# A hand-ordered three-block transformer program: one piece of filler work of each attention step is put between the turnings and the scores, and small ScalarE operations go behind the copies

## The chip, the cores and the metric

The program runs on one core of a Trainium2 chip. The metric is the device time of one execution in microseconds, less is better. TensorE (PE) does the matrix products, ScalarE (ACT) copies and exponentials, VectorE (DVE) elementwise work and reductions, GpSimd (POOL) a few additions and its own queue of transfers, SyncE (SP) issues the weights' transfers.

## The reference

Sequence 512, width 1024, everything float32. First one block, then twice the same layer:

```
first block:  ffn -> [ local attention (8 heads) | dilated attention (3 groups of 4 heads) ]
              each branch times a gate sigmoid(h @ w_gate), summed, @ w_out -> ffn
layer x 2:    h = rmsnorm(x);  z = h @ w_in
              o_c = causal attention over latents (8 heads)
              o_b = banded attention with sinks (8 heads)
              o_a = g0 * compressed attention + g1 * selected + g2 * window  (8 heads)
              g = sigmoid(h @ w_branch_gate)                      # 3 x 1024 columns
              x += (g_a*(o_a@w_a) + g_b*(o_b@w_b) + g_c*(o_c@w_c)) @ w_out
              ffn, embedding gate; at the end rmsnorm
```

## The kernel before

A planner in Python writes down a list of steps, and each engine's program is made by walking that list: an engine's instructions stand in the order of the steps, and each waits on semaphores for what it reads and for the buffer it writes. So the order in which `go()` and `layer()` call their helpers is the order on every engine.

Products of weights (`dense`) are split in float32r halves: a weight tile of 512 KB comes in on SP's queue into one of three raw tiles, ScalarE writes its high half (the CAST at L1877), VectorE the rest (L2010), into one of four split tiles, and TensorE does three matmuls for each of eight chunks, 24 matmuls of 128x512 (L1691 to L1693). The split of weight unit u+2 is listed with the first matmuls of unit u. Sums stand in PSUM banks: ring `PB` has four, taken in turn, ring `OB` four, taken oldest first.

Attention is done by `attend(slots, fill)`. It goes over pairs of slots; a slot has two batches of heads, so a step has four batches. In step p the old pair is finished and the new pair begun:

```
turn(old)      PE transposes the four score matrices (L1775) into 4 PB banks, ACT copies them out (L1937)
turned, behind things put off from the step before
score(new)     PE products (L1767) into PB banks; DVE adds the mask and takes the peak (L2083), ACT exp (L1929)
value(old)     PE products (L1789)
norm(new)      DVE divides by the sums (L2098 to L2114); the next step's turn waits for it
between(new)   post, pre, and then the step's portion of `fill`
```

The fill is what TensorE does while the softmax of the new pair runs on DVE and ACT: gates of the branch, either whole (`gates`, 24 matmuls) or in quarters (`quarters`, 6 matmuls each). A gate ends in `tangent`: DVE multiplies the bank (L2160), ACT takes the tanh (L1953), POOL's queue stores it to HBM. For a bank of `OB` this is put into `behind`, that is after the next turnings on the list; for a bank of `PB` it follows at once. `roomy()` picks the ring.

The places: local attention (`ga`, 4 steps with turnings, about 448 to 520 us), dilated groups 0, 1, 2 (`gb`, to 700 us), and in each layer the causal attention (whole gates, from 1255 and 2208 us), the band (from 1364 and 2316 us) and the last attention (from 1486 and 2439 us, eleven turnings, here called A1 to A11). In the causal one `heads_in` makes the keys and queries of the next heads in between: three products in three PB banks, copied out by ACT (L1969), and for every other head a rotation, whose first copy is L1966. In the last one `cmp_score` makes the compressed scores of the next query tile: 3 DVE operations, an exp on ACT (L1997), and 4 DVE operations (L2280 to L2286).

Of the kernel before, what the change touches and what calls it, by code (L numbers as in the profile page):

```python
# [159 lines left out]
class Plan:  # L160
# [3 lines left out]
    def __init__(self, nc, D, out):  # L164
# [9 lines left out]
        self.inside = False  # L174
        self.unopened = 0
# [332 lines left out]
    def attend(self, slots, fill=(), at_once=False):  # L508
# [6 lines left out]
        self.inside = True  # L515

# [65 lines left out]
        def between(ss):  # L582
            for f in ss:
                for B in slots[f]:
                    for U in B:
                        if U.get("post"):
                            U["post"]()
            for f in ss:
                for B in slots[f]:
                    for U in B:  # L590
                        if U.get("pre"):
                            U["pre"]()
            for f in next(fill, None) or ():
                f()

        for p in range(len(pairs) + 1):
# [6 lines left out]
            for f in back:  # L603
                f()
            if not new:
                between(())
# [31 lines left out]
    def roomy(self):  # L638
        return self.OB if self.inside and len(self.OB.out) + self.unopened < 3 else self.PB

    def quarters(self, name, ms, H):

        def piece(m, k, held):
            if k == 0:
                ring = self.roomy()
                assert ring is self.OB
# [12 lines left out]
    def tangent(self, name, m, ring, b, bank, tok):  # L659
        def tangent():  # L660
# [3 lines left out]
            self.gate_at[name, m] = (len(self.gate_at), self.load(self.D["gates"][len(self.gate_at)], s[:], (n, "t")))  # L664
            self.tmp.give(i, self.gate_at[name, m][1])
        if ring is self.OB:
            self.behind.append(tangent)
        else:
            tangent()
# [76 lines left out]
    def go(self):  # L746
# [98 lines left out]
        self.attend(self.batches(na_us), [ga[0:2], ga[2:3], ga[3:4], ga[4:6], ga[6:7]])  # L845
# [15 lines left out]
        for g in range(3):  # L861
# [22 lines left out]
            for t, hh in order:  # L884
# [35 lines left out]
            self.attend(self.batches(us), self.portions(*[(gb[0:8], (3, 2, 2, 1)), (gb[8:20], (8, 4)),  # L920
                                                          (gb[20:32], (8, 4))][g]), at_once=g > 0)
# [193 lines left out]
    def layer(self, L, xt, ht):  # L1115
# [100 lines left out]
        us = []  # L1216

        def heads_in(m, later=False, between=None):
# [15 lines left out]
            if m % 2 == 0:  # L1234
                places = to_place[m // 2] = []

                def rotated(d):
                    for f in places:
# [4 lines left out]
                          done=rotated)  # L1243
            got = []
            for R, (b, bank, tok) in ((kf, res[0]), (qf, res[1])):
# [7 lines left out]
                got.append((took, w))  # L1253
            tq = got[1][0]
# [228 lines left out]
        for qt in range(4):  # L1483
            for kind in range(2):
                for h in range(8):
# [4 lines left out]
                    def cmp_scores(qt=qt):  # L1490
# [3 lines left out]
                        OB.give(b, (n, "b"))  # L1494
# [1069 lines left out]
```

## Time and profile before

| | us |
|---|---|
| median of 3 runs | 3093.63 (3093.18 to 3093.67) |
| the profiled execution, its own time | 3091.7 |
| its span, first to last instruction | 3089.5 |
| PE busy | 3020.2 |
| DVE busy | 1672.6 |
| ACT busy | 1203.5 |
| mean granted TensorE clock | 0.996 |

The span is the time between the first and the last instruction; the 2.2 us around it are outside the program. Busy times overlap. In the waits "A <- B: x, n" says that A's engine stood idle for x us over n times until B was done. In a timeline row the bracket gives the idle time of the engine just ahead of the row and what ended it.

### The profile page before, as it was taken

To read this page: it belongs to the slowest core of one execution; us is meant where nothing else is said; L and a number is where in the kernel's file an instruction comes from. 1 tells how busy PE (TensorE), PEld (TensorE's weight loads), DVE (VectorE), ACT (ScalarE), POOL (GpSimd) and SP (SyncE) were. 2 spreads that over 40 slices of the span, in tenths; PEclk is the share of its full clock that TensorE was granted. 3 is DMA by queue.
4 is the path that set the end of the run, shared out by engine and by line. 5 is a ranking of instruction groups with operands and counts; after the bars stand their busy time and mean duration, and the time that the engine had idled before them with its cause. 6 is when DMAs were issued, how large, how long until landed. Compare 5 with 4: busy or idle time off the path is not lost.

```text
span 3089.5 us, 40035 instructions
## 1 busy us (share of the span) xinstructions
PE 3020.2 (98%) x15272; PEld 2478.8 (80%) x15272; DVE 1672.6 (54%) x3050; ACT 1203.5 (39%) x2238; POOL 286.5 (9%) x344
## 2 busy tenths in 40 slices
PE   8999999999999999999999999999999999999998
PEld 7888887888888888778778888888778778888887
DVE  6653364446565426556656555436556666555434
ACT  4322334443432224645553322224546553322223
POOL 0000110001100012011001100013111001100002
PEclk9999999999999999999999999999999999999999
DMA  5333373325233333225225332334223315322332
GB/s 170 113 96 114 108 144 119 103 86 179 95 100 99 96 108 111 73 101 167 73 63 183 97 96 96 96 98 151 87 95 117 127 49 184 103 96 96 102 97 95
DMA packets 105996, 338.15 MB, mean 109 GB/s; under 512 B 15360, under 2 KB 15888, under 8 KB 105680
## 3 DMA queue, kind: packets, MB, share of 16 engines
q1 hardware_dynamic: 84816, 272.45, 28.0%
q0 software_dynamic: 20992, 63.15, 7.0%
q8 instruction: 123, 2.02, 0.3%
q14 instruction: 65, 0.53, 0.1%
HBM read 299.24 MB, written 27.52 MB: 106 GB/s over the span
## 4 chain that ended last, share of the span: by engine, by line
PE 89%; ACT 3%; DVE 3%; issue 2%; DMA 2%; POOL 1%; SPq 0%; POOLq 0%; DVEq 0%; ACTq 0%
PE bk L1691 26%; PE bk L1693 25%; PE bk L1692 25%; PE bk L1767 3%; PE bk L1789 3%; PE bk L1775 1%; PE bk L1730 1%; PE bk L1732 1%; PE bk L1731 1%; ACT t L1929 1%; ACT t L1937 1%; ACT t L1877 1%; DMA t<-value_scratch 0%; DVE t L2160 0%; DVE t L2010 0%
## 5 line engine op out<-in xcount | busy, mean ns | idle before, releaser
L1691 PE MATMUL bk<-t,t 128*128 128x512 f32 x3784 | 1481.0, 391 | 25.1 <-DVE t L2010 13.8
L1693 PE MATMUL bk<-t,t 128*128 128x512 f32 x3784 | 1469.2, 388 | 0.0
L1692 PE MATMUL bk<-t,t 128*128 128x512 f32 x3784 | 1468.3, 388 | 0.0
L1691 PEld LDWEIGHTS bk<-t,t 128*128 128x128 f32 x3784 | 712.6, 188 | 182.1 <-issue 26.2
L1693 PEld LDWEIGHTS bk<-t,t 128*128 128x128 f32 x3784 | 712.5, 188 | 147.3
L1692 PEld LDWEIGHTS bk<-t,t 128*128 128x128 f32 x3784 | 713.1, 188 | 141.9
L2010 DVE TENSOR_TENSOR t<-t,t 128x1024 fp32r<-128x1024 f32 (+3 forms) x538 | 616.7, 1165 | 353.9 <-ACT t L1877 353.2
L1877 ACT CAST t<-t 128x1024 fp32r<-128x1024 f32 (+3 forms) x538 | 511.3, 979 | 217.1 <-PE bk L1693 109.5
L1920 ACT CAST t<-t 128x512 fp32r<-128x512 f32 x88 | 54.6, 621 | 433.7 <-DVE t L2070 433.7
L1929 ACT ACTIVATE t<-t,t 128x256 f32<-128x256 f32 (+3 forms) x336 | 173.1, 516 | 95.8 <-DVE t L2083 94.9
L2316 POOL TENSOR_TENSOR t<-t,t 128x512 f32<-128x512 f32 x58 | 78.3, 1349 | 1387.4 <-ACT t L1907 1387.3
L2067 DVE SCALAR_TENSOR_TENSOR t<-bk,t 128x512 f32<-128x512 f32 x88 | 60.6, 691 | 246.8 <-PE bk L1693 246.7
L2083 DVE CUSTOM_DVE_ANT_0 t<-bk,t 128x256 f32<-128x256 f32 (+3 forms) x272 | 110.2, 456 | 125.3 <-PE bk L1767 77.9
L1903 ACT ACTIVATE t<-t,t 128x512 fp32r<-128x512 f32 x72 | 51.0, 722 | 224.3 <-DVE t L2293 195.1
L1767 PE MATMUL bk<-t,t 64*128 64x256 f32 (+7 forms) x672 | 115.3, 421 | 20.5 <-ACT t L1937 18.4
L1917 ACT ACTIVATE t<-t 128x512 f32<-128x512 f32 x88 | 55.5, 632 | 189.8 <-DVE t L2061 189.8
L1937 ACT COPY t<-bk 128x512 f32<-128x512 f32 (+2 forms) x200 | 95.3, 558 | 64.6 <-PE bk L1775 63.9
L1767 PEld LDWEIGHTS bk<-t,t 64*128 64x128 f32 (+1 forms) x672 | 65.7, 190 | 54.2 <-ACT t L1937 39.2
L2312 POOL DMA_DIRECT2D gate_scratch<-t x64 | 35.3, 552 | 728.1 <-ACT t L1953 563.4
L1789 PEld LDWEIGHTS bk<-t,t 128*64 128x64 f32 x1456 | 79.2, 137 | 24.3 <-issue 23.6
L1775 PE MATMUL bk<-t,t 128*128 128x128 f32 x728 | 90.6, 273 | 5.3 <-ACT t L1969 4.5
L1775 PEld LDWEIGHTS bk<-t,t 128*128 128x128 f32 x728 | 82.0, 140 | 15.4 <-ACT t L1969 5.7
(173 smaller groups left out, 1997.6 us busy)
## 6 DMA issues: line engine op xcount, KB each, us to landing
t<-in_f_g SPq DMA_DIRECT2D x88, 512.0 KB, 4.4
t<-in_f_u SPq DMA_DIRECT2D x88, 512.0 KB, 3.6
t<-in_f_d SPq DMA_DIRECT2D x64, 512.0 KB, 4.3
t<-in_gate SPq DMA_DIRECT2D x48, 512.0 KB, 3.7
gate_scratch<-t POOLq DMA_DIRECT2D x64, 256.0 KB, 2.3
t<-gate_scratch POOLq DMA_DIRECT2D x64, 256.0 KB, 3.7
t<-in_f_d SPq DMA_DIRECT2D x32, 384.0 KB, 3.1
t<-in_wo SPq DMA_DIRECT2D x24, 512.0 KB, 3.7
```

Source lines behind the costliest of these rows:

```text
L1691: pe.matmul(o, wh, xh, start=start, stop=False)
L1692: pe.matmul(o, wh, xl, start=False, stop=False)
L1693: return pe.matmul(o, wl, xh, start=False, stop=stop)
L1767: ins = pe.matmul(b["bank"][:, w["at"]:w["at"] + w["w"]], w["q"], w["k"], start=True, stop=True)
L1775: ins = pe.transpose(b["bank"][:, j * 128:(j + 1) * 128], b["S"][:, j * 128:(j + 1) * 128], P.cn("ident"))
L1789: ins = pe.matmul(v["o"], v["v"][j], b["PT"][:, c:c + 128], start=j == 0 and not v["add"], stop=end, skip_group_check=v["add"])
L1877: e.then_inc(act.copy(P.spl[u % NSPL][:, 0, 0:n], P.raw[u % NRAW][:, 0:n]), "halves", ("hi", u))
L1929: e.then_inc(act.activation(S, S, ACT.Exp, bias=w["nm"], scale=-1.0, accum_out=w["sm"]), "exps", (n, "e", j, i))
L1937: e.then_inc(act.copy(b["PT"][:, 0:b["w"]], b["bank"][:, 0:b["w"]]), "acts", (n, "a", j))
L2010: e.then_inc(dve.tensor_tensor(lo, P.raw[u % NRAW][:, 0:n], hi.bitcast(F32), ALU.subtract), "rests", ("lo", u))
L2083: e.then_inc(dve.tensor_tensor_reduce(b["S"][:, c:c + k], b["bank"][:, c:c + k], w["table"], -w["scale"], w["init"], ALU.add, ALU.min, w[" ...
L2316: e.then_inc(pool.tensor_tensor(P.acc[:], P.acc[:], s["q"][:], ALU.add), "pools", (n, "p"))
```

## The change

Five edits, all of order; no instruction is added or removed.

1. In every step with an old and a new pair and more than one function in its portion, the first function is called between the turnings and the scores. Three calls of `attend` are touched by that (dilated group 0, band, last attention). In groups 1 and 2 one quarter (`lead`) is called ahead of the first scores.
2. `tangent` is two steps now. The DVE product stays where it was; the tanh and the store of a gate in a PB bank go to `behind`, after the next turnings. In the last step (`closing`) a whole gate takes a PB bank.
3. The local attention's portions are 3, 1, 1, 1, 1 gates, before 2, 1, 1, 2, 1.
4. `heads_in` lists its four copies ahead of the rotation's copy.
5. `cmp_score` is two steps: the first (transposes, 3 DVE operations, exp) stands between the norms of the new pair (`later`), the second, `cmp_share`, where all of it was.

```diff
@@ attend
+        for f in lead:
+            f()
...
             for f in back:
                 f()
+            todo = list(next(fill, None) or ())
+            if old and new and len(todo) > 1:
+                todo.pop(0)()
             if not new:
-                between(())
+                self.closing = True
+                between((), todo)
+                self.closing = False
...
             for s in old if not at_once else ():
                 done(s)
+            each(new, "later")
             for s in new[1:2]:
                 norm(s)
             if new:
-                between(new)
+                between(new, todo)
@@ roomy, tangent
-        return self.OB if self.inside and len(self.OB.out) + self.unopened < 3 else self.PB
+        return self.OB if self.inside and not self.closing and len(self.OB.out) + self.unopened < 3 else self.PB
...
             n = self.step("sigmoid", g=bank, tg=tok, s=s, f=f, r=self.rf_tok)
             ring.give(b, (n, "g"))
-            self.gate_at[name, m] = (len(self.gate_at), self.load(self.D["gates"][len(self.gate_at)], s[:], (n, "t")))
-            self.tmp.give(i, self.gate_at[name, m][1])
+
+            def turned():
+                k = self.step("tangent", s=s, t=(n, "g"))
+                self.gate_at[name, m] = (len(self.gate_at), self.load(self.D["gates"][len(self.gate_at)], s[:], (k, "t")))
+                self.tmp.give(i, self.gate_at[name, m][1])
+            if self.inside and ring is self.PB:
+                self.behind.append(turned)
+            else:
+                turned()
@@ calls
-        self.attend(self.batches(na_us), [ga[0:2], ga[2:3], ga[3:4], ga[4:6], ga[6:7]])
+        self.attend(self.batches(na_us), [ga[0:3], ga[3:4], ga[4:5], ga[5:6], ga[6:7]])
...
-            self.attend(self.batches(us), self.portions(*[(gb[0:8], (3, 2, 2, 1)), (gb[8:20], (8, 4)),
-                                                          (gb[20:32], (8, 4))][g]), at_once=g > 0)
+            self.attend(self.batches(us), self.portions(*[(gb[0:8], (3, 2, 2, 1)), (gb[9:20], (7, 4)),
+                                                          (gb[21:32], (7, 4))][g]), at_once=g > 0, lead=[[], gb[8:9], gb[20:21]][g])
@@ heads_in
-            if m % 2 == 0:
+            def turning():
...
+            if m % 2 == 0 and not later:
+                turning()
             got = []
...
                 got.append((took, w))
+            if m % 2 == 0 and later:
+                turning()
```

**The order on ScalarE at the end of the causal attention of layer 0.** The last exponentials of the fifth step, the split of a weight unit, the tanh of the gate, and the copies of the last turnings (tiles `t_76` to `t_79`). Before:

```order
L1929 ACTIVATE t_79,t_66<-t_79,t_66 128x512
L1877 CAST t_58<-t_54 128x1024
L1953 ACTIVATE t_72<-t_72 128x512
L1937 COPY t_76<-bk 128x256
L1937 COPY t_77<-bk 128x256
L1937 COPY t_78<-bk 128x512
L1937 COPY t_79<-bk 128x512
L1923 CAST t_129<-bk 128x4x128 x2
L1877 CAST t_55<-t_52 128x1024
```

Of the change:

```order
L1959 ACTIVATE t_79,t_66<-t_79,t_66 128x512
L1907 CAST t_58<-t_54 128x1024
L1967 COPY t_76<-bk 128x256
L1967 COPY t_77<-bk 128x256
L1967 COPY t_78<-bk 128x512
L1967 COPY t_79<-bk 128x512
L1953 CAST t_129<-bk 128x4x128 x2
L1983 ACTIVATE t_72<-t_72 128x512
L1907 CAST t_55<-t_52 128x1024
```

The tanh has moved from ahead of the four copies to behind them and behind the output's two halves (line numbers differ by 30).

**The order on ScalarE at A1 of layer 0.** The exp of the compressed scores (L1997, then L2027), copies of the turnings, the tanh of the gate finished just before (`t_70`), the split of the unit that belongs to the moved quarter (`t_57`), the new pair's exponentials. Before:

```order
L1997 ACTIVATE t_69<-t_69 128x256
L1877 CAST t_56<-t_54 128x1024
L1937 COPY t_76<-bk 128x512
L1937 COPY t_77<-bk 128x512
L1937 COPY t_78<-bk 128x512
L1937 COPY t_79<-bk 128x512
L1953 ACTIVATE t_70<-t_70 128x512
L1929 ACTIVATE t_74,t_66<-t_74,t_66 128x256 x2
L1929 ACTIVATE t_75,t_66<-t_75,t_66 128x256 x2
L1929 ACTIVATE t_76,t_66<-t_76,t_66 128x256 x2
L1929 ACTIVATE t_77,t_66<-t_77,t_66 128x256 x2
L1923 CAST t_131<-bk 128x4x128
```

Of the change:

```order
L2027 ACTIVATE t_68<-t_68 128x256
L1907 CAST t_56<-t_54 128x1024
L1967 COPY t_76<-bk 128x512
L1967 COPY t_77<-bk 128x512
L1967 COPY t_78<-bk 128x512
L1967 COPY t_79<-bk 128x512
L1983 ACTIVATE t_70<-t_70 128x512
L1907 CAST t_57<-t_52 128x1024
L1959 ACTIVATE t_74,t_66<-t_74,t_66 128x256 x2
L1959 ACTIVATE t_75,t_66<-t_75,t_66 128x256 x2
L1959 ACTIVATE t_76,t_66<-t_76,t_66 128x256 x2
L1959 ACTIVATE t_77,t_66<-t_77,t_66 128x256 x2
```

The CAST of `t_57`, before behind these exponentials and an output, now stands ahead of them. VectorE's rest of `t_57` likewise moves ahead of the peaks.

**The order on TensorE at A2 of layer 0.** The last filler matmuls ahead of the turnings, the turnings, the scores, the compressed values. Before:

```order
L1692 MATMUL bk<-t_50,t_55 128x512
L1693 MATMUL bk<-t_50,t_55 128x512
L1775 MATMUL bk<-t_59,t_74 128x128 x4
L1775 MATMUL bk<-t_59,t_75 128x128 x4
L1775 MATMUL bk<-t_59,t_76 128x128 x4
L1775 MATMUL bk<-t_59,t_77 128x128 x4
L1767 MATMUL bk<-t_149,t_161 128x256 x8
L1861 MATMUL bk<-t_71,t_160 64x128 x8
```

Of the change:

```order
L1805 MATMUL bk<-t_59,t_76 128x128 x4
L1805 MATMUL bk<-t_59,t_77 128x128 x4
L1721 MATMUL bk<-t_50,t_55 128x512
L1722 MATMUL bk<-t_50,t_55 128x512
L1723 MATMUL bk<-t_50,t_55 128x512
L1721 MATMUL bk<-t_50,t_55 128x512
L1722 MATMUL bk<-t_50,t_55 128x512
L1723 MATMUL bk<-t_50,t_55 128x512
L1797 MATMUL bk<-t_149,t_161 128x256 x8
L1891 MATMUL bk<-t_71,t_160 64x128 x8
```

A quarter of a gate, six matmuls, stands between the turnings and the scores; 12 of the 18 filler matmuls remain ahead of the next turnings.

## Rows read from the trace of the kernel before

**Rows 1.** The page's part 1: busy time, share, count of each engine.
```profile
PE 3020.2 (98%) x15272; PEld 2478.8 (80%) x15272; DVE 1672.6 (54%) x3050; ACT 1203.5 (39%) x2238; POOL 286.5 (9%) x344
```

**Rows 2.** Waits of TensorE over the span: engine, line waited for: us, times, longest.
```profile
PE bk L1767 <- ACT t L1937: 18.4, 19, 3.2
...
PE bk L1691 <- ACT t L1923: 5.5, 2, 2.8
```

**Rows 3.** Timeline of one local-attention step; columns: start, us, engine, line.
```profile
461.36 1.91 PE L1775 MATMUL bk<-t,t 128*128 128x128 f32 x16
...
462.29 0.63 ACT L1953 ACTIVATE t<-t 128x512 f32<-128x512 f32 x1 [3.58 <-DVE t L2160]
462.82 2.03 ACT L1937 COPY t<-bk 128x512 f32<-128x512 f32 x4
...
464.02 1.42 PE L1767 MATMUL bk<-t,t 64*128 64x256 f32 x9 [0.75 <-ACT t L1937]
```

**Rows 4.** Timeline where the first step's values wait for their operand.
```profile
470.18 0.66 PE L1789 MATMUL bk<-t,t 128*64 128x128 f32 x8 [2.58 <-DMA t<-value_scratch]
```

**Rows 5.** Windows: length, PE busy (matmuls), granted clock, DMA share, GB/s.
```profile
471.40:474.80 3.40, 3.40 (x10) 0.50 0.28 64
...
1498.80:1505.60 6.80, 5.89 (x36) 0.50 0.34 118
2451.50:2458.30 6.80, 5.88 (x70) 1.00 0.30 116
2198.50:2202.00 3.50, 3.50 (x10) 0.51 0.54 192
1247.40:1250.90 3.50, 3.50 (x17) 1.00 0.61 190
```

**Rows 6.** Timeline of the last causal turning, layer 0.
```profile
1325.82 0.63 ACT L1953 ACTIVATE t<-t 128x512 f32<-128x512 f32 x1 [3.99 <-DVE t L2160]
...
1327.83 1.11 ACT L1923 CAST t<-bk 128x512 fp32r<-128x512 f32 x2
...
1329.27 0.47 PE L1691 MATMUL bk<-t,t 128*128 128x512 f32 x1 [2.77 <-ACT t L1923]
```

**Rows 7.** Timeline of the causal step that has heads_in(2), layer 0.
```profile
1274.76 0.58 ACT L1966 COPY t<-bk 128x512 f32<-128x512 f32 x1 [1.62 <-PE bk L1693]
1275.24 2.44 ACT L1969 ACTIVATE t<-bk 64x512 f32<-64x512 f32 x4
...
1277.78 1.06 PE L1775 MATMUL bk<-t,t 128*128 128x128 f32 x8 [0.60 <-ACT t L1969]
```

**Rows 8.** Timeline at the start of the second dilated group.
```profile
623.83 1.39 PE L1767 MATMUL bk<-t,t 64*128 64x128 f32 x20 [0.73 <-DVE t L2050]
```

**Rows 9.** Timeline of two band steps, layer 0.
```profile
1386.49 1.91 PE L1775 MATMUL bk<-t,t 128*128 128x128 f32 x16
...
1388.35 2.11 PE L1767 MATMUL bk<-t,t 64*128 64x256 f32 x16
...
1397.87 1.91 PE L1775 MATMUL bk<-t,t 128*128 128x128 f32 x16
...
1398.31 0.62 DVE L2112 TENSOR_SCALAR t<-t,t 128x256 f32<-128x256 f32 x2
```

**Rows 10.** Timeline of the first two steps of the last attention, layer 1.
```profile
2449.82 0.42 ACT L1997 ACTIVATE t<-t 128x256 f32<-128x256 f32 x1 [2.84 <-DVE t L2278]
2450.14 1.03 ACT L1877 CAST t<-t 128x1024 fp32r<-128x1024 f32 x1
...
2452.41 2.12 PE L1767 MATMUL bk<-t,t 64*128 64x256 f32 x16 [3.16 <-ACT t L1937]
...
2453.55 0.43 DVE L2083 CUSTOM_DVE_ANT_0 t<-bk,t 128x256 f32<-128x256 f32 x1 [0.17 <-PE bk L1767]
...
2461.29 0.73 DVE L2114 TENSOR_SCALAR t<-t,t,t 128x256 f32<-128x256 f32 x2
```

**Rows 11.** Waits of TensorE, 2440 to 2560 us (last attention, layer 1).
```profile
PE bk L1767 <- ACT t L1937: 5.4, 3, 3.2
```

More of the change, by code:

```diff
@@ L580, in norm, with each, between @@
                 X["p"] = (k, "d")
-        def between(ss):
-            for f in ss:
-                for B in slots[f]:
+        def each(ss, name):
+            for s in ss:
+                for B in slots[s]:
                     for U in B:
[L586 to L593, printed above, removed]
+                        if U.get(name):
+                            U[name]()
+        def between(ss, todo):
+            each(ss, "post")
+            each(ss, "pre")
+            for f in todo:
                 f()
+            todo.clear()
         for p in range(len(pairs) + 1):
@@ L659, in tangent, with left @@
     def tangent(self, name, m, ring, b, bank, tok):
-        def tangent():
+        def left():
             i, s, f = self.tmp.take()
@@ L1494, in cmp_scores, with cmp_shares @@
                         OB.give(b, (n, "b"))
+                        cmp_[qt] = (i, S, n)
+                    def cmp_shares(qt=qt):
+                        i, S, n = cmp_[qt]
+                        n = self.step("cmp_share", qt=qt, S=S, e=(n, "e"), sgs=sgs, sgt=sgt)
                         cmp_[qt] = (i, S, (n, "d"))
@@ L1521, in post, with later @@
                             f_(qt + 1)
+                    def later(qt=qt, kind=kind, h=h, f_=cmp_scores):
+                        if h == 0 and kind == (qt > 0) and qt < 3:
+                            f_(qt + 1)
                     if qt == 0 and kind == 0 and h == 0:
-                        first_scores = cmp_scores
+                        first_scores = (cmp_scores, cmp_shares)
                     def done(tok, es, qt=qt, kind=kind, h=h):
@@ L1542, in layer @@
                                                        for j in range(qt + 1)],
-                        lambda: v_t, h, qt, 0.125, col, open=opn, post=post, done=done, most=4, add=True, gate=gate,
+                        lambda: v_t, h, qt, 0.125, col, open=opn, post=post, later=later, done=done, most=4, add=True, gate=gate,
                         sms=columns(S_SM, col, 1), rss=columns(S_RS, col, 1),
                         o=lambda qt=qt, h=h: half_out(obk[qt][1], h), ot=lambda qt=qt: obk[qt][2]))
-        first_scores()
+        for f in first_scores:
+            f()
         opened[14]()
@@ L2278, in vector @@
             vec(dve.tensor_tensor(S3, S3, mx.unsqueeze(2).broadcast_to([128, 8, 32]), ALU.subtract), (n, "s"))
-            e.wait_ge((n, "e"))
+        elif kind == "cmp_share":
+            qt = s["qt"]
+            S3 = s["S"][:, 0:256].rearrange("p (h n) -> p h n", h=8)
+            some = P.cn("cmp01")[:, qt:qt + 1]
+            sx = P.st[:, 176:184]
+            e.wait_ge(s["e"])
             vec(dve.tensor_reduce(sx, S3, AX, ALU.add), (n, "1"))
```

20 lines of the change are left out of this document (10 added, 10 removed).

## Prediction

> **What bounds the kernel now.** I read the page's busy times first. TensorE is busy 3020.2 of the span of 3089.5 us, VectorE little more than half, ScalarE 39% [rows 1]. So nothing but TensorE's idle time, under 70 us, and stretches at a lower clock can be won by an edit that only changes order. The Trainium skill ("Perfetto Trace Analysis", Identifying the Most-Contended Engine) warns that matmul busy time says little of the distance from the roofline, and names the busy share of the weight loads instead, here 80%. For what order alone can win I keep to the idle time.
>
> Then the waits of TensorE: the largest is 18.4 us in 19 waits, scores (L1767) waiting for ScalarE's copies of the turned scores (L1937), since four turnings fill the four banks of `PB` and the scores need two of them. 5.5 us in two waits are matmuls of L1691 behind an output's split (L1923) [rows 2]. Then the timelines at each place touched.
>
> **How a step is reckoned.** Let s be how much later (plus) or earlier the scores of a step start than before. A moved quarter is 6 matmuls, 1.36 us: 0.227 us from start to start in the fuller timeline, and the window at full clock has 17 in 3.5 us [rows 5]. From start of turnings to start of scores a step takes 1.86 us [rows 9], of which the turnings are 1.64 and the wait and switch 0.22. With a quarter in between, the turnings' end and the scores are 1.50 apart. TensorE then comes to the next turnings 1.36 earlier relative to s. If the norms are ready, that is gain; if not, it waits again. So every moved quarter wins the gap less 0.14, and loses what the next norms are late.
>
> **The terms.**
>
> *Tanh behind the copies.* In a local step the tanh takes 462.29 to 462.82 after waiting for VectorE's product, then come the copies; scores start 2.66 us after the turnings [rows 3], against 1.86 where no tanh stands ahead [rows 9]. That is 0.80 us a step. It holds in three local steps with scores, and in two steps of each causal attention: 7 x 0.8 = 5.6. Ahead of the fourth local turnings' gate I take another 0.3. What is late next are the exponentials, by one tanh; they have cover, since these steps still have a whole gate, 24 matmuls, ahead of the next turnings.
>
> *The last gate of the causal attention.* The gate waits 2.77 us for the output's split, which frees an `OB` bank; that split starts at 1327.83 behind tanh and copies [rows 6]. In a `PB` bank it needs only the first copy. 2.8 a layer, 5.6.
>
> *The rotation behind the four copies.* ScalarE sits idle 1.62 us until the third product ends, copies it, and only then spends 2.44 us on the four copies of the first two; the turnings wait, at the last 0.60 us, for those banks [rows 7]. Moved ahead, two copies fall into that idle time. The third bank comes free last, with one copy of 0.58 and a product on VectorE of about the same, so I count 1.4 a layer, 2.8.
>
> *Three gates in the first local step.* The values of the next step waited 2.58 us for `value_scratch`, until 470.18 [rows 4]. With one gate more ahead of them, 5.45 us, they come later than that. Right behind the wait the granted clock was 0.50 for 3.4 us [rows 5], which cost about 1.5. Together 4.1. The fourth step loses the gate, where the norms have been ready 7 us before; no loss.
>
> *Leads.* The first scores of groups 1 and 2 wait 0.73 for a product on VectorE [rows 8]; covered: 1.5.
>
> *Dilated group 0.* Gaps of 0.45 give s = +1.1, then +0.9; the third turnings' norms, ready now just in time, are then late. Net loss 0.4.
>
> *Band.* Here gaps are 0.22, so s = +1.3. At the second turnings VectorE had been busy until the scores and takes up 1 us of that. At the third it had waited for them: all 1.2 us of delay arrive. The last norm there runs 1398.31 to 1398.93, its turnings begin 1.3 us after 1397.87 [rows 9], so there were 0.25 us of slack. The turnings end 1.0 late, and after the last moved quarter 0.9 is left: loss 1.8 in two layers.
>
> *Last attention.* Scores wait 5.4 us a layer for copies, the longest 3.2 [rows 11]; with waits too short for that view the gaps are 8.1, less 10 x 0.14: 6.7 could be won. At A1 the exp of the compressed scores starts at 2449.82, after all norms, a cast of 1.03 follows, then the copies; scores only at 2452.41 [rows 10]. Now the exp can start near 2447.2; the three operations put between the norms cost the last norm about 1.0 and the turnings' end 0.5; scores start near 2451.0, s = -1.4. But VectorE's rest of the moved quarter's weight unit stands ahead of the peaks, and waits for the chain product L2160 (end 2452.5), tanh 0.6, cast 1.0; with its own 1.15 the peaks start at 2455.3, before at 2453.55. From there to the end of the last norm, 2461.29 + 0.73 [rows 10], were 8.5 us, 1.5 of them a wait for values which now is gone, so about 7.4: 2462.7. TensorE is at the turnings near 2458.9, waits in between them, and ends them where it did, -0.15. The gain of A1 is eaten. A2: s = +1.1, plus three compressed operations between the norms: A3's turnings end 0.9 late; its gap of 1.9 gives s = +0.5. A4 to A10 win their gaps, but at A6 the norms are 0.65 late, since a weight unit's split was moved ahead of the peaks at A5. Sum at A11: -1.8 a layer, 3.6. In layer 0 the wait of A1 was followed by a granted clock of 0.50 for 6.8 us, 36 matmuls instead of the 70 of layer 1 in the same stretch of the program [rows 5]; without a wait of 3.2 us in one piece it goes: 2.7 more.
>
> Sum of gains: 5.6 + 0.3 + 5.6 + 2.8 + 4.1 + 1.5 + 3.6 + 2.7 = 26.2; losses 0.4 + 1.8 = 2.2. Net 24.0. The profiled span of 3089.5 becomes 3065.5. That execution's own time, 3091.7, stands 1.9 under the median of 3093.6, so I predict 3093.6 - 24 = 3069.6, that is 3070.
>
> **Bounds of what is unseen.** For each norm chain the ends are: no waits for norms at all, and every moved quarter paid back in full at the next turnings. The first is 13 us better than my sum (6.7 a layer for 1.8 in the last attention; 1.5 a layer in the band; 0.5 in group 0, rounded down). The second is the rival on the other side. I stand between, nearer to no wait for late steps, where the norms were ready a microsecond or two before, and with full waits at A2, A3 and the band's third.
>
> **Rivals.**
>
> *The softmax keeps up everywhere.* For it: VectorE waits for scores or values in nearly all these steps, so it has time. Against: the last norm of the band ends within 0.3 us of its need [rows 9]. 3070 - 13 = 3057. Chance 0.12.
>
> *The clock.* The same wait of the same program in two layers ended near 2198 and near 1247; the one was followed by a granted clock of 0.51 for 3.5 us and 10 matmuls, the other by 1.00 and 17 [rows 5]. So whether a short stop costs half speed is a matter of when it falls. All stops now fall about 7 to 20 us earlier. If A1's half clock stays and one more stop of about 2 us catches one: +2.7 + 1.6, 3074. The Trainium skill ("TensorE: Matmul & The Clock Gate", What's actually happening) has it that the array runs at half clock unless recent activity released it, and that the observation runs free of the kernel; by that rule equal stops may differ, and the two layers agree. By it alone no half-clock stretch could be booked as won, and the sum would be 19.8 in place of 24. Chance 0.14.
>
> *The tanh was not what held the copies.* If the copies start no earlier, 5.9 us of gain fall away: 3076. Against: steps without a tanh ahead are shorter by just that. Chance 0.06.
>
> *Slower: every turning waits for its norms.* The mechanism is the fill taken from ahead of the turnings. 28 quarters of 1.36 us are moved, 38 us of cover. If all of it came back as waits at the next turnings, it would meet 37 us of gains (24 and the 13 above): 3095. If the weight splits moved ahead of the exponentials (three a layer and the two leads) cost 2.2 us of cast and rest each as well, 15 to 20 us more: 3110. It decides from the point at which norms were ready less than 1.36 us ahead; in the last attention's late steps they were ready 1.4 to 2.4 ahead by the timeline, and only the band and A1 to A3 are short. Chance 0.04 for slower, 0.05 for an outcome within 0.2% (6 us, about what a measurement of this kernel can tell).
>
> **Numbers.** My forecast, 3070 with its own range of 3064 to 3076, has 0.59. The range takes in the clock and the tanh rivals and part of the full gain: 3061 to 3079. Faster 0.91, within 0.2% 0.05, slower 0.04.
>
> **What would show it.** Right: the wait of scores for copies falls from 18.4 to under 5 us; the wait for `value_scratch` and the one of 2.77 us vanish; seven local and causal steps take 1.86 from turnings to scores. New: waits of the turnings (L1775 of before) for VectorE's norms, 2 to 3 us at A2 and about 1 at A3 and the third band turning, some 9 to 12 us in all; ScalarE's cast ahead of the exponentials at A1, A5, A9. Wrong: if A2's turnings don't wait, the time is nearer to 3060; if A4 to A11 wait too, nearer to 3085; a granted clock of 0.5 in more than two stretches inside the span adds 1.6 each.

## The result, and the profile after

The changed kernel takes 3071.4 us (median of four, 3068.3 to 3072.6), the kernel before on the same chip 3093.4: a ratio of 0.9928, interval 0.9910 to 0.9945, 22.0 us less. The profiled execution took 3072.1 us, its span is 3070.0, 19.5 less than before's. Busy times have hardly moved against [rows 1], so what was won is, by the sums, idle time of TensorE. (Counts by engine are the same as before; of the instructions outside these counts, such as waits and register work, the profile has 5 more, 40040 for 40035 in all, so "no instruction is added" holds for the working ones.)

```profile
PE 3019.5 (98%) x15272; PEld 2473.5 (81%) x15272; DVE 1670.5 (54%) x3050; ACT 1206.1 (39%) x2238; POOL 287.1 (9%) x344
```

The waits of TensorE over the span; line numbers of the programs of the engines are 30 higher than before, so L1797 is the scores, L1805 the turnings, L1819 the values, L1967 the copies of the turnings, L1983 the tanh:

```profile
PE bk L1805 <- DVE t L2128: 6.9, 11, 1.4
...
PE bk L1805 <- DVE t L2323: 2.6, 6, 0.6
...
PE bk L1797 <- ACT t L1967: 2.2, 4, 0.7
...
PE bk L1819 <- DMA t<-value_scratch: 0.6, 1, 0.6
```

The wait of scores for copies is 2.2 us in place of 18.4, the one for an output's split is gone from the list [rows 2]. In their place stand waits that before had hardly at all: turnings (L1805) that wait for VectorE's norms, 6.9 us, and for a copy on VectorE (L2323, the turned compressed scores out of their bank), 2.6. Half of the latter, 1.3 us, is the wait of A1's turnings. The kernel with edit 5 and no moved quarter has it too, before has not: it is edit 5's and not the moved quarters'.

Where the 19.5 us come from can be read by setting the starts of the same turnings of both traces side by side. "Won in the stretch" is what the stretch that ends at that row won; the last column is the prediction's.

| turnings | before | after | earlier by | won in the stretch | predicted |
|---|---|---|---|---|---|
| start of the local attention (first scores) | 448.33 | 449.40 | -1.1 | -1.1 | - |
| dilated group 0, first | 579.57 | 573.63 | 5.9 | 7.0 | 6.8 |
| (scores of group 1) | 622.61 | 618.73, behind a lead of 1.36 | 5.2 | -0.7 | -0.4 |
| causal, layer 0 | 1263.40 | 1256.06 | 7.3 | 2.1 | 1.5 |
| band, layer 0 | 1372.87 | 1359.32 | 13.5 | 6.2 | 5.8 |
| band's last | 1410.98 | 1398.80 | 12.2 | -1.4 | -0.9 |
| A1, layer 0 | 1494.64 | 1482.02 | 12.6 | 0.4 | 0 |
| A11, layer 0 | 1602.67 | 1587.86 | 14.8 | 2.2 | 4.5 |
| causal, layer 1 | 2215.98 | 2200.84 | 15.1 | 0.3 | 0 |
| band, layer 1 | 2325.50 | 2304.15 | 21.4 | 6.2 | 5.8 |
| band's last | 2363.61 | 2343.66 | 20.0 | -1.4 | -0.9 |
| A1, layer 1 | 2447.34 | 2427.39 | 20.0 | 0 | 0 |
| A11, layer 1 | 2552.65 | 2533.42 | 19.2 | -0.7 | 1.8 |

Up to the first band turnings of layer 0 the sum holds within 0.6 us a row. The first 1.1 us are lost in the first 16 us of the program, which is the same in both: from 12 to 16 us TensorE did 11 matmuls after the change, 15 before. Since the program is the same there, I put it down to the execution and not to the change.

In the timeline of the first local step the tanh (ScalarE, L1983) is behind the four copies, and the scores come 1.85 us behind the turnings, where they came 2.66 behind them [rows 3]; in the values' wait 0.62 us are left of 2.58 [rows 4]:

```profile
467.87 1.91 PE L1805 MATMUL bk<-t,t 128*128 128x128 f32 x16
...
468.50 2.05 ACT L1967 COPY t<-bk 128x512 f32<-128x512 f32 x4 [9.93 <-PE bk L1805]
469.72 2.11 PE L1797 MATMUL bk<-t,t 64*128 64x256 f32 x16
...
470.42 1.70 ACT L1983 ACTIVATE t<-t 128x512 f32<-128x512 f32 x3
...
473.92 0.66 PE L1819 MATMUL bk<-t,t 128*64 128x128 f32 x8 [0.62 <-DMA t<-value_scratch]
```

The last causal turning of layer 0: the gate follows the turnings at once, against 2.77 us in [rows 6], and the output's split no longer stands in its way:

```profile
1314.37 1.60 PE L1805 MATMUL bk<-t,t 128*128 128x128 f32 x12
...
1315.73 0.48 PE L1721 MATMUL bk<-t,t 128*128 128x512 f32 x1
...
1316.49 1.08 ACT L1953 CAST t<-bk 128x512 fp32r<-128x512 f32 x2
```

The step with heads_in(2): ScalarE no longer idles for the third product before it makes its copies, and the turnings end 1.3 us sooner than in [rows 7]. What is late now is the rotation's product on VectorE (L2245), which frees the third bank:

```profile
1267.21 1.64 PE L1805 MATMUL bk<-t,t 128*128 128x128 f32 x12
1268.15 0.59 ACT L1996 COPY t<-bk 128x512 f32<-128x512 f32 x1
...
1268.77 0.69 DVE L2245 TENSOR_TENSOR t<-bk,t 128x512 f32<-128x512 f32 x1 [1.29 <-ACT t L1996]
1269.61 0.63 PE L1805 MATMUL bk<-t,t 128*128 128x128 f32 x4 [0.75 <-DVE t L2245]
```

The third band turnings, in place of the unbroken ones of [rows 9]: the second half waits for a norm:

```profile
1384.26 1.28 PE L1805 MATMUL bk<-t,t 128*128 128x128 f32 x8
...
1386.24 1.35 PE L1805 MATMUL bk<-t,t 128*128 128x128 f32 x8 [0.69 <-DVE t L2128]
```

And A1 and A2 of layer 1, beside [rows 10]. L2040 is VectorE's rest of a weight unit, L2113 the peaks:

```profile
2431.76 2.00 PE L1797 MATMUL bk<-t,t 64*128 64x256 f32 x16
...
2432.78 0.63 ACT L1983 ACTIVATE t<-t 128x512 f32<-128x512 f32 x1 [1.72 <-DVE t L2190]
2433.31 1.03 ACT L1907 CAST t<-t 128x1024 fp32r<-128x1024 f32 x1
...
2434.38 1.23 DVE L2040 TENSOR_TENSOR t<-t,t 128x1024 fp32r<-128x1024 f32 x1 [1.63 <-ACT t L1907]
2435.52 0.41 DVE L2113 CUSTOM_DVE_ANT_0 t<-bk,t 128x256 f32<-128x256 f32 x1
...
2442.21 0.63 PE L1805 MATMUL bk<-t,t 128*128 128x128 f32 x4 [1.39 <-DVE t L2128]
2443.30 1.12 PE L1805 MATMUL bk<-t,t 128*128 128x128 f32 x4 [0.46 <-DVE t L2323]
```

The trace is 20.0 us ahead of before's at A1, so the scores' 2431.76 is 2451.7 in before's time, 0.7 sooner than 2452.41 and with a quarter more done. The peaks start 3.76 us behind them, 1.1 us in [rows 10], because the unit's rest stands ahead of them and waits, product (L2190) to tanh to cast, 1.63 us. The turnings of A2 wait twice. And right behind the second wait the clock falls (the last four turnings and the quarter run at half clock, 1.2 GHz for 2.4); windows of after, columns as in [rows 5], at A2 of layer 0, A2 of layer 1, and a stretch near 2184:

```profile
1498.00:1501.50 3.50, 3.50 (x12) 0.56 0.00 0
2443.50:2447.00 3.50, 3.50 (x12) 0.57 0.02 5
2184.00:2187.50 3.50, 3.50 (x10) 0.55 0.51 155
```

### The profile page after: what moved, and what is told of

Read it like the earlier page. It is cut to its first block, busy times and chain, and to the rows that moved or that the text cites. A ratio compares the mean times of both kernels' runs of the same rounds, so it can differ in the third digit from the quotient of the medians.

```text
span 3070.0 us, 40040 instructions
## 1 busy us (share of the span) xinstructions
PE 3019.5 (98%) x15272; PEld 2473.5 (81%) x15272; DVE 1670.5 (54%) x3050; ACT 1206.1 (39%) x2238; POOL 287.1 (9%) x344
## 4 chain that ended last, share of the span: by engine, by line
PE 87%; DVE 4%; ACT 4%; issue 2%; DMA 2%; POOL 1%; SPq 0%; DVEq 0%; POOLq 0%; ACTq 0%
PE bk L1721 25%; PE bk L1723 25%; PE bk L1722 25%; PE bk L1797 3%; PE bk L1819 2%; PE bk L1805 2%; ACT t L1959 1%; PE bk L1760 1%; PE bk L1761 1%; PE bk L1762 1%; DVE t L2040 1%; ACT t L1907 1%; DMA t<-value_scratch 1%; DMA t<-in_gate 0%; PE bk L1773 0%
## 5 line engine op out<-in xcount | busy, mean ns | idle before, releaser
L2040 DVE TENSOR_TENSOR t<-t,t 128x1024 fp32r<-128x1024 f32 (+3 forms) x538 | 615.7, 1163 | 367.8 <-ACT t L1907 367.5
L2113 DVE CUSTOM_DVE_ANT_0 t<-bk,t 128x256 f32<-128x256 f32 (+3 forms) x272 | 109.9, 456 | 109.2 <-PE bk L1797 70.4
L1967 ACT COPY t<-bk 128x512 f32<-128x512 f32 (+2 forms) x200 | 98.2, 557 | 86.7 <-PE bk L1805 84.6
L1797 PE MATMUL bk<-t,t 64*128 64x256 f32 (+7 forms) x672 | 110.1, 409 | 2.2 <-ACT t L1967 2.2
L1805 PE MATMUL bk<-t,t 128*128 128x128 f32 x728 | 97.7, 276 | 13.3 <-DVE t L2128 6.9
L1805 PEld LDWEIGHTS bk<-t,t 128*128 128x128 f32 x728 | 81.9, 141 | 30.4 <-issue 15.7
L1819 PEld LDWEIGHTS bk<-t,t 128*64 128x64 f32 x1456 | 78.8, 137 | 22.4 <-issue 21.7
L1797 PEld LDWEIGHTS bk<-t,t 64*128 64x128 f32 (+1 forms) x672 | 64.3, 187 | 35.9 <-issue 18.6
```

The costliest lines, as they stand in the source:

```text
L1797: ins = pe.matmul(b["bank"][:, w["at"]:w["at"] + w["w"]], w["q"], w["k"], start=True, stop=True)
L1805: ins = pe.transpose(b["bank"][:, j * 128:(j + 1) * 128], b["S"][:, j * 128:(j + 1) * 128], P.cn("ident"))
L1819: ins = pe.matmul(v["o"], v["v"][j], b["PT"][:, c:c + 128], start=j == 0 and not v["add"], stop=end, skip_group_check=v["add"])
L1967: e.then_inc(act.copy(b["PT"][:, 0:b["w"]], b["bank"][:, 0:b["w"]]), "acts", (n, "a", j))
L2040: e.then_inc(dve.tensor_tensor(lo, P.raw[u % NRAW][:, 0:n], hi.bitcast(F32), ALU.subtract), "rests", ("lo", u))
L2113: e.then_inc(dve.tensor_tensor_reduce(b["S"][:, c:c + k], b["bank"][:, c:c + k], w["table"], -w["scale"], w["init"], ALU.add, ALU.min, w[" ...
```

## The experiments

All were timed beside the kernel before, four or five executions each, the two single edits that come out near before eleven. The medians of before in the three sets were 3092.5, 3092.3 and 3091.3 us (single executions from 3087.6 to 3099.1). The first set is the runs that put one place back, the third the two with a quarter at A1 alone, edit 4 alone and the leads, which ran on another chip of the kind; all others are in the second. The text gives differences of medians as they are. Where they go across sets they are good to about 1 us: counted from each set's own before, a run of the first set comes out 0.9 us slower against the change, one of the second 1.1 (none moved is then 13.7 and not 14.8 us under the change), and one of the third 1.0 slower against none moved. `keep` names steps whose quarter stays behind the scores.

### One place of the change put back

**The quarter at A1 put back.**

```diff
+    def attend(self, slots, fill=(), at_once=False, lead=(), keep=()):
+            if old and new and len(todo) > 1 and p not in keep:
                 todo.pop(0)()
@@ last attention
+                    (4, 3, 3, 3, 3, 3, 3, 3, 3, 3, 3, 2)), keep=(1,))
```

> The change, with the quarter at A1 of both layers put back behind the scores; all else as in the change. Theory 1 (the moved quarter opens a gate, so the cast and the rest of a weight unit stand ahead of the peaks, behind product, tanh and cast; the peaks of A1's new pair start 2 us late, A2's turnings wait for norms, and a stretch of half clock follows): the peaks come before 2.5 us behind the start of the scores, A2's turnings wait under 0.5 us in place of 1.9 in layer 1, the half clock behind them goes, and the time falls by 4 to 7 us from the change's 3071.4 to about 3066. Theory 2 (it is the three compressed operations between the norms that make A2 late): the waits at A2 stay, and the time falls by 1 us at most. Theory 3 (the half clock behind A2 falls at a moment of its own): the waits go, the half clock stays somewhere near, the time falls by 2 to 3 us.

3062.4 us, ratio to before 0.9906 (0.9891 to 0.9921), 9 less than the change and below the expected 3066. In layer 1 the scores start at 2424.19, the first peak at 2426.49, 2.3 behind; the turnings of A2 run through:

```profile
2424.19 2.00 PE L1797 MATMUL bk<-t,t 64*128 64x256 f32 x16
...
2426.49 0.42 DVE L2113 CUSTOM_DVE_ANT_0 t<-bk,t 128x256 f32<-128x256 f32 x1
...
2433.28 1.91 PE L1805 MATMUL bk<-t,t 128*128 128x128 f32 x16
```

From A1 to A11 each layer is 4.0 us shorter than in the change: 2.9 at the end of A2's turnings, 1.1 in the quarter behind them, which ran at half clock. These 8 us in two layers are more than the 4 to 7 expected. Theory 1 holds in its mechanism, theory 2 is out, and of theory 3 nothing is seen here; that the half clock needs more than these waits is shown two runs further on. Read in windows of 3.5 us, no stretch between the start-up and the end has a granted clock under 0.97 in this profile, so the stretch near 2184 is gone too (1.7 us); that part of the 9 the theory had not promised.

**All ten quarters of the last attention put back** (`keep=range(1, 11)`).

> The change, with all ten quarters of each last attention put back behind the scores (A1 to A10), the compressed scores still split in two. Theory 1 (moved quarters are worth only their gap less 0.14 us, and lose it where norms are late): A4 to A10 gained 0.4 us in all in the change, A2 and A3 lost 2.5; with none moved, the gaps of A1 and A3 are closed already by the earlier exp, so the time is that of the run with A1 alone put back or 1 to 2 us less, 3064 to 3066. Rival (the quarters at A4 to A10 do win their gaps, 2.3 us a layer, and only A1 harms): 3 to 5 us more than with A1 alone put back, about 3070.

3059.0 us, ratio 0.9891 (0.9878 to 0.9905), 12.3 less than the change and below what was expected. By the starts of A11 each layer is 5.0 us shorter than in the change, 0.95 more than with A1 alone put back. So the quarters at A2 to A10, taken together, lose: with the earlier exp there is no gap left that they could fill (without them scores follow the end of these turnings after 0.2 to 0.4 us).

**The quarters of group 0 and of the band put back** (`keep=(1, 2, 3)` in both calls; it touches two quarters of the group and three of each band).

> The change, with the quarters of the band (three in each layer) and of the first dilated group (three) put back behind the scores. Theory: there the scores came 0.22 us behind the turnings anyway, so a quarter ahead of them only delays the softmax; the band's third turnings no longer wait (1.4 us a layer) and the third of the group neither (0.9, against gaps of 0.45): 3.4 us less than the change, 3068. Rival (the waits of those turnings come from earlier scores of the step before and stay): no difference.

3064.5 us, ratio 0.9910 (0.9896 to 0.9923), 6.9 less than the change. By the traces group 0 gives 0.7 and each band 1.4, 3.5 us where 3.4 was forecast; the time fell by twice that. Most of the rest is clock, 1.4 us in each layer from A1 to A11: the waits at A2 are all still there, 1.39 and 0.46 us as in the change, but no half clock follows them. Its timeline and window in layer 1:

```profile
2435.01 0.63 PE L1805 MATMUL bk<-t,t 128*128 128x128 f32 x4 [1.39 <-DVE t L2128]
2436.09 0.66 PE L1805 MATMUL bk<-t,t 128*128 128x128 f32 x4 [0.46 <-DVE t L2323]
```

```profile
2436.50:2440.00 3.50, 3.50 (x26) 1.00 0.02 5
```

The quarter behind them takes 1.56 us from its first matmul to the scores (2436.51 to 2438.07), in the change 2.70 (2444.06 to 2446.76). Equal stops, other clock.

**The compressed scores in one piece** (edit 5 undone, all else as in the change).

```diff
-                    def later(qt=qt, kind=kind, h=h, f_=cmp_scores):
-                        if h == 0 and kind == (qt > 0) and qt < 3:
-                            f_(qt + 1)
...
-                    def post(qt=qt, kind=kind, h=h, f_=cmp_shares, g_=cmp_turn):
+                    def post(qt=qt, kind=kind, h=h, e_=cmp_scores, f_=cmp_shares, g_=cmp_turn):
...
                         if h == 0 and kind == (qt > 0) and qt < 3:
+                            e_(qt + 1)
                             f_(qt + 1)
```

> The change, with the compressed scores in one piece behind both norms as before (edit 5 undone). Theory 1 (the late step is that of the peaks at A1, set by the unit's rest behind product, tanh and cast): the exp and with it the copies of A1 come 1 to 1.5 us later, scores wait again 1 to 2 us there and at A3, while the turnings of A1 no longer wait 1.1: the time is within 3 us of the change, rather above, 3071 to 3074. Theory 2 (the three operations between the norms make A2 and A3 late): the waits of A2 fall by over 1 us a layer and the time to 3068 or less.

3072.8 us, ratio 0.9934 (0.9922 to 0.9947), 1.5 more than the change. The scores wait for copies again:

```profile
PE bk L1795 <- ACT t L1965: 9.0, 8, 1.8
```

(2.2 in the change), and the turnings wait less for norms, 3.4 us for 6.9. From A1 to A11 the two layers are 0.4 and 0.5 us shorter, so inside the steps the two sides nearly balance. The change carries its half clock behind A2 in that; beside the run before this one, which has edit 5 and none of that half clock, both layers here are 1.0 and 0.9 us longer, so at a like clock edit 5 wins a little even with the quarters moved. What puts the time above lies outside them, mainly between group 2 and the causal attention, where the trace loses 3.7 us with two stretches of low clock (near 700 and 1243) that the change's profile doesn't have. The size is theory 1's, and the time forecast by theory 2 is out. A part of its mechanism is there: the waits of A3's turnings, 0.79 us for a norm and 0.22 for a norm's last product (L2144) in layer 1 of the change, are gone here, so the three operations between the norms do have a share in them. At A2 of layer 1 both waits stayed.

### No quarter moved at all

**None moved**: both of the edits above, leads and edits 2 to 5 kept.

> The change without any quarter moved ahead of the scores (dilated group 0, the band and the last attention all as before in that), but with the two leads and edits 2 to 5. Theory 1 (each moved quarter is worth its gap less 0.14 us at best, and norms that come late take that back): the two losses measured apart, 12.3 us in the last attention and about 3.5 in band and group (6.9 came out, some 3 of it from stretches of half clock behind A2 that this kernel no longer has a wait for), add up to 15 to 16: 3055 to 3057. Rival (the two overlap, since part of what the band's quarters cost is taken up by waits later on): 3058 or more.

3056.6 us, ratio 0.9884 (0.9870 to 0.9897): 14.8 less than the change, near the 15 to 16 that were added up. It is the fastest kernel of this study. Its waits of TensorE in the last attention of layer 1, beside 5.4 us in [rows 11]:

```profile
PE bk L1805 <- DVE t L2323: 0.6, 1, 0.6
```

The change had 4.0 there (2.5, 1.3 and 0.2 in three lines). No stretch of half clock is left in the profile.

**The same, compressed scores in one piece.**

> As the run without any quarter moved, and the compressed scores in one piece behind both norms as before (edit 5 undone). With no quarter in between, the scores of A1 and A3 wait for the copies behind the exp again: 3.2 and 1.7 us and 0.6 at A6 a layer, as before the change, while the turnings of A1 lose their wait of 1.1. Theory (edit 5 is what closes these gaps): 3 to 5 us a layer more than with the split, 3062 to 3066, one stretch of half clock more or less in it. Rival (the norms are the chain that counts and give it back at A2): within 2 us.

3069.9 us (3064.5 to 3073.4), ratio 0.9928 (0.9915 to 0.9940): 13.3 more, more than expected. The old gap is there in full:

```profile
PE bk L1795 <- ACT t L1965: 5.5, 3, 3.2
```

From A1 to A11 a layer is 7.3 us longer than with the split in layer 0 and 4.5 in layer 1: 3.2 at A1, 1.7 at A3, 0.6 at A6, less 1.1 of A1's turnings, and two windows of low clock in layer 0 (1488 and 1513). Outside, clock stretches near 700, 1241 and 2188 come on top; the profiled execution, the longest of the five, has all of them and is 17.1 us longer than that of none moved, where the medians are 13.3 apart. So edit 5 is worth 9 to 13 us if no quarter stands between (4.5 us a layer in the steps, 13.3 in the time), and 1.5 us in the time if one does, which is no more than such a difference is good for: both fill the same gap.

**One moved again, at A1**, the first quarter of its gate.

> The kernel without any moved quarter, and one moved again: that at A1 of both layers, the first of a gate, which brings the cast and the rest of a weight unit ahead of the peaks. Theory 1 (that split is what makes the peaks late): the peaks start 3.5 us or more behind the start of the scores, the turnings of A2 wait 1.5 to 2 us and end 2.9 us later than with none moved: 6 to 8 us in two layers, with or without a stretch of half clock behind, 3062 to 3065 against 3056.6. Rival (a quarter between turnings and scores costs its own 1.4 us at the next norms, whatever it brings): the same time as the run with a plain quarter there.

3063.3 us, ratio 0.9906 (0.9892 to 0.9919), 6.7 more than with none. The unit's rest waits, the peaks start 3.77 us behind the scores, both waits of A2's turnings are back. In layer 1:

```profile
2422.32 2.00 PE L1797 MATMUL bk<-t,t 64*128 64x256 f32 x16
...
2424.95 1.23 DVE L2040 TENSOR_TENSOR t<-t,t 128x1024 fp32r<-128x1024 f32 x1 [1.63 <-ACT t L1907]
...
2426.09 0.42 DVE L2113 CUSTOM_DVE_ANT_0 t<-bk,t 128x256 f32<-128x256 f32 x1
...
2432.78 0.63 PE L1805 MATMUL bk<-t,t 128*128 128x128 f32 x4 [1.39 <-DVE t L2128]
```

**One moved at A1, but the second quarter of its gate.**

```diff
-                    (4, 3, 3, 3, 3, 3, 3, 3, 3, 3, 3, 2)), keep=range(2, 11))
+                    (5, 3, 3, 3, 3, 3, 3, 3, 3, 3, 3, 1)), keep=range(2, 11))
```

> As the run with A1's quarter alone moved, but each portion of the last attention begins one quarter later (5, 3, 3, ..., 3, 1 in place of 4, 3, 3, ..., 3, 2), so that the quarter moved at A1 is the second of its gate and brings no split. Theory 1: the first peaks follow the scores as soon as these are there (1 us), the chain is late by the quarter's own 1.4 us less the slack there was, A2's turnings wait 0.5 to 1 us: 3058 to 3060. Rival (any quarter there costs the same): within 1.5 us of the run with the first quarter of a gate there.

3058.9 us, ratio 0.9890 (0.9875 to 0.9905), 2.3 more than with none, and in the same set 4.4 less than with the first quarter, so the rival is out. The peaks start 1.85 us behind the scores, since two rests run back to back ahead of them, but neither waits; A2's turnings wait 0.46 us for L2323 and not for a norm:

```profile
2422.97 2.36 DVE L2040 TENSOR_TENSOR t<-t,t 128x1024 fp32r<-128x1024 f32 x2
2423.99 2.00 PE L1797 MATMUL bk<-t,t 64*128 64x256 f32 x16
...
2425.84 0.42 DVE L2113 CUSTOM_DVE_ANT_0 t<-bk,t 128x256 f32<-128x256 f32 x1
```

So the quarter that brings a split costs two to three times the one that doesn't (6.7 against 2.3; counted from each set's own before, 7.7 against 3.3). One thing is not kept equal: the first portion has a quarter more here, which also takes away the 1.1 us that A1 loses to its turnings' wait. Layer 0, where none of the three profiles has low clock between A1 and A11, allows for it: from A1 to A11 it takes 100.83 us with none, 103.30 with the first quarter and 100.47 with the second. With the 1.1 put back, the second costs 0.7 us there and the first 2.5.

### Single edits on the kernel before

**Edit 2 alone** (tanh behind the copies; a `PB` bank for the last whole gate).

> The kernel before with edit 2 alone: the tanh of gates in PB banks behind the next copies, and a PB bank for the last whole gate. From the trace of the change: 0.8 us in each of two local steps with scores (the third, behind the third gate, not counted) up to three, 0.4 at the fourth, 0.8 in two steps and 3.0 at the last gate of each causal attention: 2.8 + 9.2 = 12.0 less than before, 3080.5. Rival (part of it needs the other edits, since only three of the local steps' tanhs stand ahead of copies with the gates as before): 3082 to 3084.

3080.6 us, ratio 0.9961 (0.9947 to 0.9975), 11.8 less than before; 12.0 was expected. All three local steps and two causal steps a layer are 0.8 shorter, each last causal gate 3.0. Its first local step, scores 1.86 behind the turnings:

```profile
462.50 1.91 PE L1785 MATMUL bk<-t,t 128*128 128x128 f32 x16
463.14 2.05 ACT L1947 COPY t<-bk 128x512 f32<-128x512 f32 x4 [6.09 <-PE bk L1785]
...
464.36 0.92 PE L1777 MATMUL bk<-t,t 64*128 64x256 f32 x6
```

**Edit 3 alone** (local portions 3, 1, 1, 1, 1).

> The kernel before with edit 3 alone: local portions of 3, 1, 1, 1, 1 gates. Theory: the wait for the value operand goes from 2.6 to 0.6 us, and the half clock of 3.4 us behind it with it (1.5): 3.5 less than before, 3089. Rival 1 (the half clock stays or moves): 2 less, 3090.5. Rival 2 (the fourth step, with one gate in place of two, waits for its norms, and nothing is won): 3092 or more.

3090.4 us, ratio 0.9993 (0.9984 to 1.0002), 1.9 less; the interval holds no change. In its profile the wait for `value_scratch` is gone altogether, the half clock behind it too, and the local attention is 4.5 us shorter than before's. It has four stretches of low clock (near 1244, 1328, 1502, 2452), where before has three (the one removed, one near 1502 and one near 2199), and its whole span is only 0.1 us shorter than before's. The one behind the first wait for an output's split, where before's clock stayed at 1.00:

```profile
1326.50:1330.00 3.50, 2.94 (x7) 0.50 0.05 15
```

**Edit 4 alone** (copies ahead of the rotation).

> The kernel before with edit 4 alone: the four copies of heads_in ahead of the rotation's copy. Theory, from the change's trace: the turnings of that step take 2.7 in place of 4.0 us, the scores come 0.25 sooner behind them: 1.5 us a layer, 3.0 in all, 3089.4 against before's 3092.4. Rival (the rotation's late product delays the keys of the next heads and gives it back): 3092.

3093.2 us, ratio 1.0005 (0.9996 to 1.0013): no gain to be seen in the time. The step itself is as forecast, 1.5 us shorter in each layer, turnings to scores 2.86 in place of 4.36:

```profile
1275.26 1.65 PE L1779 MATMUL bk<-t,t 128*128 128x128 f32 x12
1277.66 0.63 PE L1779 MATMUL bk<-t,t 128*128 128x128 f32 x4 [0.76 <-DVE t L2219]
1278.12 1.03 PE L1771 MATMUL bk<-t,t 128*128 128x256 f32 x4
```

But the clock falls behind both waits of 2.8 us for the output's split, where before it stayed at 1.00:

```profile
1328.00:1331.50 3.50, 3.07 (x8) 0.53 0.09 12
2276.30:2279.80 3.50, 3.23 (x8) 0.57 0.08 13
```

The span of the profiled execution is 1.6 us shorter than before's; why the median of the others is not, no trace shows.

**The leads taken out** of the kernel with none moved (portions 8, 4).

> The kernel without any moved quarter and without the two leads either (dilated groups 1 and 2 with portions 8, 4 as before). Theory: the scores of both groups wait 0.7 us for a product on VectorE again, and the step costs 1.0 us each in all as in the trace of the change: 2.1 us more than with the leads, 3058.7. Rival (the leads only move the wait to the next turnings): the same as with them, 3056.6.

3061.4 us, ratio 0.9898 (0.9885 to 0.9912), 4.8 more than with them, where 2.1 were expected. The wait is back (616.80, below), each group is 1.0 us longer, as forecast; 3.4 more come between the groups and the causal attention, in two stretches of low clock, where the kernel with leads has 1.00:

```profile
616.80 1.83 PE L1797 MATMUL bk<-t,t 64*128 64x128 f32 x28 [0.72 <-DVE t L2080]
```

```profile
700.00:703.50 3.50, 3.50 (x27) 0.58 0.31 123
1242.50:1246.00 3.50, 3.50 (x11) 0.61 0.57 181
```

## Why the prediction was right, and where not

*Tanh behind the copies*: right, 0.8 us in each of seven steps, also alone on the kernel before. *The last causal gate*: right, 3.0 for 2.8. *The rotation*: right in the step, 1.5 for 1.4, with the third bank's product as what is late next. *Three gates first*: right, except that 0.6 us of the wait for `value_scratch` stayed; the local attention won 7.0 for 6.8. *Leads*: 1.0 each where 0.75 was booked. *Group 0 and band*: sign and place right, undersized: 0.7 for 0.4, and 1.4 for 0.9 a band, since I took 0.25 us of slack at the third turnings and a last moved quarter that gives 0.1 back.

*The last attention* is the step of the sum that failed. I booked 3.6 us and 2.7 of clock; the change brought 2.2 in layer 0 and -0.7 in layer 1, 1.5 together. Three things were mis-sized. The peaks were forecast for 2455.3 on before's clock and came at 2435.52 + 20.0 = 2455.5, the last norm for 2462.7 and came at 2442.91 + 20.0 = 2462.9: this part was right. But the turnings' end does not hang on that norm alone. Behind it on VectorE stands the copy L2323, which frees the bank that the last four turnings write; they waited 0.46 us for it, and the end came 0.7 us late where I had 0.15 early. Then the quarter behind those waits ran at half clock in both layers, 1.1 us: I had weighed "A1's half clock stays and one more stop catches one" at 0.14, and it went from A1 but came behind A2. Both made the scores of A2 late, and with these A3's norms: its turnings ended 3.1 us late in layer 1, where I had 0.9. From there on A4 to A10 were to win their gaps; they won 0.4 in layer 1, and with all quarters put back that stretch is no longer (67.8 us for 67.9), so none of it came from their quarters.

The rule "a moved quarter wins the gap less 0.14 and loses what the norms are late" held, but I applied it to gaps that edit 5 closes by itself. I credited both edits with the same 3.2 and 1.7 us. Taken apart, edit 5 alone is worth 9 to 13 us, and the moved quarters, with the half clock behind their waits, cost 14 to 15.

*The rivals*: the clock's took place in part: A1's half clock went, one came behind A2 in each layer, and the stretch near 2184 is the one that before has near 2199. The tanh one is out: the copies started 0.6 us behind the turnings. The slower one had its mechanism at A2 and A3, the third band turnings and the group's, with 0.8 and 0.4 us more at A6 and A8; the turnings of A4, A5, A7 and A9 to A11 did not wait. Of the splits moved ahead of the exponentials, A1's cost most, A5's shows in the 0.8 of A6, A9's not at all.

*The number*: 3070 for 3071.4, but not by its own sum, and that it comes so near is in part luck. The span fell by 19.5 where 24.0 was forecast: 4.8 less came in the last attention, 1.3 less in group 0 and the bands, 1.1 less through the start-up; 2.6 more came elsewhere (0.8 in the causal attentions, 0.6 from the leads, 0.2 locally, 1.0 in stretches that the change doesn't touch). The median fell by 22.0, since before's profiled execution happened to be 1.7 us under the median of 3093.4 and that of after 0.7 over. For the execution that the sum was made for, the forecast span of 3065.5 came out 4.5 us short. The new waits of turnings, forecast as 9 to 12 us, were 9.9: 6.9 and 0.4 for norms, 2.6 for L2323, which I had not named; 0.4 of the waits for norms before had too. Low clock was found in three stretches, one more than I allowed for.

What stays open: which stops the clock answers. The Trainium skill ("TensorE: Matmul & The Clock Gate", What's actually happening) has the array at half clock unless recent activity released it; that the same waits at A2 are followed by 0.57 in one kernel and by 1.00 in another fits the part of it by which the observation runs free of the kernel, and no run here tells more.

## What to carry to other kernels

Before a piece of filler is moved in front of dependent work, ask what else closes that gap: two edits for one gap are not added, and the one that takes away the cause (an exp that starts sooner) leaves the cover where it was: here it alone did the work, and the filler in the same gap only cost. Look at what a piece brings along on the other engines: six matmuls moved cost 2.3 us in the time when they were a gate's second quarter and 6.7 when they were its first and put a weight split ahead of the peaks. And follow the last wait to its end: the turnings needed a norm and a free bank, and the bank came later.

## What the hardware showed that I had not expected

The clock weighs as much as a single edit here. Read in windows of 3.5 us, three profiles have no stretch of low clock between start-up and end: A1 put back, all of the last attention put back, none moved. Turnings and scores wait 0.8 us at most in them. But so they do in the kernel without leads and in the one with the second quarter at A1, and these have two stretches each. Before and the five kernels in which scores wait 1.8 to 3.2 us for copies have three to six such stretches, of about 1 to 3 us each; the change has three, the other four kernels one or two. That is a tendency over fourteen profiles, not a cause that was shown: near 1328 the clock stayed at 1.00 behind a wait of 2.77 us before, and fell to 0.53 behind the same wait with edit 4. It is likely why edits whose steps got 3.0 and 4.5 us shorter measured as nothing and as 1.9, while the kernel with none moved, free of such stretches, is 35.7 us faster than before by the medians of its set.
